# Another order of the mixer steps on three engines, with 63 filler matmuls at three steps in place of 39 at two

## The reference, cut to what matters

```python
for l in range(DEPTH):                       # DEPTH = 2
    x = x + 0.5 * swiglu(rms_norm(x, ffn1_norm[l]), ...)
    h = rms_norm(x, mix_norm[l])
    pa, pb, pc, pd = jnp.split(h @ w_in[l], IN_SPLITS, axis=-1)
    ya = neighbourhood_mixer(pa, ...)        # A: 4 heads of 64, bias table
    yb = mla_mixer(pb, ...)                  # B: low-rank q and kv, 4 heads of 96, rotary
    yc = diff_mixer(pc, ...)                 # C: 4 pairs of heads of 32, softmax1 - lambda * softmax2
    yd = gqa_mixer(pd, ...)                  # D: 4 heads of 64 over 2 kv heads, rotary
    x = x + jnp.concatenate([ya, yb, yc, yd], axis=-1) @ w_out[l]
    x = x + 0.5 * swiglu(rms_norm(x, ffn2_norm[l]), ...)
    x = rms_norm(x, final_norm[l])
```

## Time and profile before

| | |
|---|---|
| median of 3 runs | 1285.97 us (1278.35, 1285.97, 1286.76) |
| the profiled execution | 1278.74 us |
| its span in the trace | 1276.5 us |
| TensorE busy | 1242.9 us, 97% |
| VectorE busy | 847.6 us, 66% |
| ScalarE busy | 640.1 us, 50% |
| first mixer stage | 192.8 to 325.3 us |
| second mixer stage | 691.0 to 823.5 us |

### The profile page before, as it was taken

One profiled execution on the slowest core, in us unless ns is written; L12 is line 12 of the kernel. 1 busy time (PEld: TensorE's weight loads), 2 busy tenths in 40 slices (PEclk: granted clock), 3 DMA queues, 4 the chain that ended last, 5 costly groups with the idle time before them and its releaser, 6 DMA issues.

```text
span 1276.5 us, 24950 instructions
## 1 busy us (share of the span) xinstructions
PE 1242.9 (97%) x10579; PEld 1218.0 (95%) x10579; DVE 847.6 (66%) x1076; ACT 640.1 (50%) x857; POOL 79.6 (6%) x57
## 2 busy tenths in 40 slices
PE   7999999999999999999999999999999999999997
PEld 7999999889999999999999998999999999899996
DVE  6766667697766666876667678776666764446666
ACT  5343346766533334533335776643333554756543
POOL 1110011210000000000001121000000000000000
PEclk9999999999999999999999999999999999999999
DMA  8876565422466665565565532365555655324543
GB/s 286 244 227 209 197 233 155 133 100 67 136 229 197 197 197 165 179 215 189 190 219 160 167 111 68 100 220 190 188 193 197 192 180 179 119 82 155 177 150 115
DMA packets 171899, 220.34 MB, mean 173 GB/s; under 512 B 5360, under 2 KB 152560, under 8 KB 171696
## 3 DMA queue, kind: packets, MB, share of 16 engines
q1 hardware_dynamic: 168064, 213.66, 52.2%
q0 software_dynamic: 2080, 2.48, 1.1%
q10 hardware_dynamic: 1680, 3.13, 0.8%
HBM read 218.15 MB, written 3.42 MB: 174 GB/s over the span
## 4 chain that ended last, share of the span: by engine, by line
PE 86%; DVE 7%; ACT 5%; issue 2%; DMA 0%; SPq 0%; DVEq 0%; POOLq 0%; POOL 0%; ACTq 0%
PE pj L485 13%; PE pj L489 13%; PE pj L488 13%; PE acc L485 7%; PE acc L489 7%; PE acc L488 7%; PE tr L485 6%; PE tr L489 6%; PE tr L488 6%; PE acc L694 2%; ACT w_hi L974 1%; PE acc L663 1%; DVE w_lo L1291 1%; PE tr L653 1%; PE tr L686 1%
## 5 line engine op out<-in xcount | busy, mean ns | idle before, releaser
L1291 DVE TENSOR_TENSOR w_lo<-raw,w_hi 128x2048 fp32r<-128x2048 f32 (+1 forms) x205 | 457.3, 2231 | 228.2 <-ACT w_hi L974 226.6
L974 ACT ACTIVATE w_hi<-raw 128x2048 fp32r<-128x2048 f32 (+1 forms) x205 | 379.3, 1854 | 382.9 <-PE pj L485 136.4
L485 PE MATMUL pj<-hT_hi,w_hi 128*128 128x256 f32 x1056 | 294.4, 279 | 0.7 <-DVE scratch L1682 0.6
L489 PE MATMUL pj<-hT_hi,w_lo 128*128 128x256 f32 x1056 | 292.3, 277 | 0.0
L488 PE MATMUL pj<-hT_lo,w_hi 128*128 128x256 f32 x1056 | 292.2, 277 | 0.0
L485 PEld LDWEIGHTS pj<-hT_hi,w_hi 128*128 128x128 f32 x1056 | 198.5, 188 | 3.9 <-issue 2.4
L488 PEld LDWEIGHTS pj<-hT_lo,w_hi 128*128 128x128 f32 x1056 | 198.4, 188 | 0.3 <-issue 0.2
L489 PEld LDWEIGHTS pj<-hT_hi,w_lo 128*128 128x128 f32 x1056 | 198.3, 188 | 0.0
L485 PE MATMUL acc<-act_hi,w_hi 128*128 128x256 f32 x704 | 194.5, 276 | 2.9 <-issue 1.5
L488 PE MATMUL acc<-act_lo,w_hi 128*128 128x256 f32 x704 | 194.3, 276 | 0.0
L489 PE MATMUL acc<-act_hi,w_lo 128*128 128x256 f32 x704 | 194.3, 276 | 0.0
(11 more groups left out here) (223 smaller groups left out, 1872.6 us busy)
## 6 DMA issues: line engine op xcount, KB each, us to landing
raw<-in_w_in SPq DMA_DIRECT2D x47, 1024.0 KB, 5.4
raw<-in_ffn_w_down SPq DMA_DIRECT2D x44, 1024.0 KB, 5.0
raw<-in_ffn_w_gate SPq DMA_DIRECT2D x43, 1024.0 KB, 5.3
raw<-in_ffn_w_up SPq DMA_DIRECT2D x43, 1024.0 KB, 5.4
raw<-in_w_out SPq DMA_DIRECT2D x12, 1024.0 KB, 5.1
raw<-in_w_proj_a SPq DMA_DIRECT2D x4, 512.0 KB, 3.5
raw<-in_w_proj_b SPq DMA_DIRECT2D x4, 512.0 KB, 3.5
raw<-in_w_proj_c SPq DMA_DIRECT2D x4, 512.0 KB, 3.5
```

Source lines behind the costliest of these rows:

```text
L485: ins = pe.matmul(out, lhs[0], rhs[0], start=first, stop=False, **kw)
L489: return pe.matmul(out, lhs[1], rhs[0], start=False, stop=last, **kw)
L974: act.activation(w_hi[r % RING][:, 0:w], raw[r % RING][:, 0:w], ACT.Copy).then_inc(hi_set, 1)
L1291: dve.tensor_tensor(w_lo[r % RING][:, 0:w], raw[r % RING][:, 0:w], w_hi[r % RING][:, 0:w].bitcast(F32), ALU.subtract).then_inc(lo_set, 1)
```

## The change

The three tables list the same steps in another order, and `BUSY` has other entries. No step is added or dropped except fillers: 26 before `pv 4` (21 before), 10 before `probs 5` (none before), and 27 before `wout 0` (18 before), so 63 per layer in place of 39. The two layers share the tables, so 48 fillers are added in all.

```diff
-         ("latent", 0), ("proj", 6), ("proj", 2), ("probs", 0), ("latent_up", 0), ("probs", 1), ("pv", 0),
...
+         ("proj", 5), ("latent", 0), ("proj", 2), ("probs", 0), ("probs", 1), ("latent_up", 0), ("pv", 0),
...
-         ("probs", 5), ("yturn", "A"), ("pv", 5), ("score", 6), ("score", 7), ("turn", "D"), ("wout", 0),
...
+         ("probs", 5), ("yturn", "A"), ("pv", 5), ("score", 6), ("score", 7), ("wout", 0), ("turn", "D"),
...
-BUSY = {('pv', 4): 21, ('wout', 0): 18}
+BUSY = {('pv', 4): 26, ('probs', 5): 10, ('wout', 0): 27}
```

More of the change, by code:

```diff
@@ L62 @@
          ("norm", "B"), ("norm", "yA"), ("norm", "D"), ("norm", "yB"), ("norm", "yC"), ("norm", "yD")]
[L68 to L76, removed]
-             ("ahead", ("wout", 0)), ("norm", "yC"), ("score", 8), ("score", 9), ("probs", 8), ("probs", 9),
-             ("yturn", "C"), ("ahead", ("wout", 1)), ("norm", "yD"), ("yturn", "D"), ("ahead", ("wout", 2))]
@@ L79 @@
[L79 to L85, removed]
-             ("soft", 5), ("yturn", "A"), ("pv", 5), ("score", 6), ("norm", "yB"), ("score", 7), ("soft", 6),
-             ("prep", "yB"), ("soft", 7), ("pv", 6), ("pv", 7), ("yturn", "B"), ("score", 8), ("score", 9),
-             ("wadd", 0), ("norm", "yC"), ("prep", "yC"), ("ahead", ("wout", 0)), ("yturn", "C"), ("soft", 8),
-             ("soft", 9), ("ahead", ("wout", 1)), ("pv", 8), ("pv", 9), ("norm", "yD"), ("prep", "yD"), ("wadd", 1),
-             ("yturn", "D"), ("ahead", ("wout", 2))]
@@ L94 @@
-BUSY = {('pv', 4): 21, ('wout', 0): 18}
+ORDER_ACT = [("ahead", ("proj", 0)), ("proj", 0), ("ahead", ("proj", 1)), ("ahead", ("proj", 4)), ("proj", 1),
+             ("norm", "A"), ("proj", 4), ("ahead", ("proj", 3)), ("proj", 3), ("norm", "latent"),
+             ("ahead", ("proj", 6)), ("turn", "A"), ("proj", 6), ("ahead", ("proj", 5)), ("score", 0), ("score", 1),
+             ("proj", 5), ("latent", 0), ("norm", "C"), ("ahead", ("proj", 2)), ("proj", 2), ("probs", 0),
+             ("ahead", ("latent_up", 0)), ("latent_up", 0), ("probs", 1), ("turn", "C"), ("norm", "B"),
+             ("ahead", ("proj", 7)), ("score", 2), ("score", 3), ("proj", 7), ("ahead", ("proj", 8)),
+             ("ahead", ("proj", 9)), ("proj", 8), ("norm", "yA"), ("probs", 2), ("proj", 9), ("probs", 3),
+             ("turn", "B"), ("norm", "D"), ("score", 4), ("score", 5), ("probs", 4), ("probs", 5), ("yturn", "A"),
+             ("norm", "yB"), ("score", 6), ("score", 7), ("turn", "D"), ("probs", 6), ("probs", 7), ("yturn", "B"),
+             ("ahead", ("wout", 0)), ("norm", "yC"), ("score", 8), ("score", 9), ("probs", 8), ("probs", 9),
+             ("ahead", ("wout", 1)), ("yturn", "C"), ("norm", "yD"), ("ahead", ("wout", 2)), ("yturn", "D")]
@@ new lines @@
+ORDER_DVE = [("means", 0), ("ahead", ("proj", 0)), ("ahead", ("proj", 1)), ("ahead", ("proj", 4)), ("norm", "A"),
+             ("prep", "A"), ("norm", "latent"), ("ahead", ("proj", 3)), ("ahead", ("proj", 6)), ("score", 0),
+             ("score", 1), ("soft", 0), ("prep", "latent"), ("latent", 0), ("norm", "C"), ("soft", 1),
+             ("ahead", ("proj", 5)), ("prep", "C"), ("ahead", ("proj", 2)), ("ahead", ("latent_up", 0)), ("pv", 0),
+             ("pv", 1), ("score", 2), ("score", 3), ("norm", "B"), ("ahead", ("proj", 7)), ("soft", 2), ("soft", 3),
+             ("prep", "B"), ("ahead", ("proj", 8)), ("pv", 2), ("norm", "yA"), ("ahead", ("proj", 9)),
+             ("norm", "D"), ("pv", 3), ("score", 4), ("score", 5), ("prep", "D"), ("prep", "yA"), ("soft", 4),
+             ("soft", 5), ("pv", 4), ("pv", 5), ("score", 6), ("yturn", "A"), ("score", 7), ("norm", "yB"),
+             ("soft", 6), ("prep", "yB"), ("soft", 7), ("yturn", "B"), ("pv", 6), ("pv", 7), ("score", 8),
+             ("score", 9), ("norm", "yC"), ("wadd", 0), ("ahead", ("wout", 0)), ("soft", 8), ("prep", "yC"),
+             ("ahead", ("wout", 1)), ("soft", 9), ("pv", 8), ("yturn", "C"), ("pv", 9), ("norm", "yD"),
+             ("prep", "yD"), ("yturn", "D"), ("ahead", ("wout", 2)), ("wadd", 1)]
```

6 lines of the change are left out of this document (3 added, 3 removed).

## The result

The changed kernel takes 1293.37 us (median of five runs, 1292.95 to 1301.39) where the kernel before, run beside it, takes 1285.97 (1278.35 to 1286.76). The ratio is 1.0097, with a 95% interval of 1.0061 to 1.0133: slower, by about 1%. The profiled execution of the changed kernel is one of the long ones, 1300.54 us.

What follows compares the result with a forecast made beforehand. TensorE, busy 97%, was taken as the bound, with VectorE setting the pace mid-stage. Terms sum to +4.7 us per stage, +9.4 on 1278.74 (1288.1, factor 1.0074); times the median 1285.97 gives 1295 us, range 1280 to 1302.

Steps and rivals of the forecast that it cites:

- Slower by less than 1%: The forecast case for the whole kernel: 1295 us, 1291 to 1300, chance 0.50.
- Point 1: Front, up to scores 2 and 3: probs 1 waits for banks, latent_up waits less; +0.4 us, between 0 and +0.8.
- Point 2: turn B: probs 3 now stands ahead and its bank must be copied by ScalarE, +0.5; turn B starts +0.9 us late.
- Point 3: VectorE's stretch to prep yA: norm B and norm D now stand in it, so yturn A starts +2.9 us late.
- Point 4: Fillers at pv 4 and probs 5: covered by TensorE's wait for prep yA, taken as 0; uncovered 0.4 + 1.2 us.
- Points 5 and 6: yturn A to wout 0 and turn D, delay +3.5 us; then probs 6 waits for banks, +0.5, so pv 6 +4.0.
- Point 7: score 8 waits for pv 6's output behind yturn B on VectorE, +0.6 us; wout 1 waits some 0.1 for wout 0's addition.
- the signs that the prediction named: Profile signs: yturn A waits 1 us or more, starts 2 to 3.5 late; probs 1 waits; stage 137.2 us; clock 1.00.
- signs of being wrong: VectorE gaps over 2 us between first C score and prep D, no wait after the 10 fillers, or any clock fall.
- not slower: Rival: yturn A does not wait for VectorE, added VectorE work costs nothing; about -0.5 us per stage, 1285 us, chance 0.20.
- Higher runs cured by fillers: Rival: something in the mixer stages makes the slower runs and more fillers prevent it; 1288 us, chance 0.18.
- The clock falls: Rival: a longer stretch of transposes and small matmuls from turn B drops the clock; +5.4 us more per stage, 1306, chance 0.12.

Runs made afterwards that it cites:

- e1: Changed kernel with VectorE's means of slot 0 put back behind the low part of projection 0: ratio 1.0109, stage 138.07 and 137.77 us.
- e3: Changed kernel with pv 3 put back ahead of norm D and prep yA between scores 4 and 5 on VectorE: ratio 1.013, stage 139.11 and 138.77 us.
- e4: Changed kernel with the old fillers (21 at pv 4, none at probs 5, 18 at wout 0): ratio 1.0124, stage 138.71 and 142.08 us.
- e5: Changed kernel with what e1, e3 and e4 put back, all at once: ratio 1.0093, stage 135.88 and 135.73 us.
- wadd_prep: Changed kernel with VectorE's wadd 0 ahead of norm yC and prep yC directly behind that norm: ratio 1.0118, stage 138.50 and 138.19 us.
- e2: Changed kernel with the addition of wout 0 put back ahead of norm yC on VectorE: 1309.63 us, ratio 1.0212, stage 143.20 and 144.93 us.
- e7: Kernel before with no fillers at all: ratio 1.01, stage 138.65 and 136.35 us.
- before_fill_0: Kernel before with no fillers at wout 0, the 21 at pv 4 kept: ratio 1.0054, stage 136.28 and 136.45 us.
- e6: Kernel before with only the new fillers (26 at pv 4, 10 at probs 5, 27 at wout 0): ratio 1.0037, stage 133.87 and 134.07 us.
- e8: Kernel before with VectorE's means 0 moved ahead of the low part of projection 0: ratio 1.0005, stage 132.69 and 132.60 us.
- late_old: e5 with turn D also ahead of wout 0, and VectorE's yturn B and steps behind score 9 in old order: ratio 1.0064, stage 135.87 and 135.64 us.

## Why the prediction was right, and where its sum was short

Slower by less than 1% was the likeliest case of the prediction, and its 1295 stands beside a measured median of 1293.4. The sum behind it was short all the same: +4.7 per stage where 7.0 and 6.7 were measured, 9.4 in all against 13.7. Two of its terms were put at nothing or next to it, the wait for `prep A` at `turn A` and the wait for the addition at `wout 1`. That the number still came out is luck: the median of the shown runs of before, 1285.97, is of the upper level and the median of the changed kernel's is of its lower one, which took away about as much as the sum missed. By the lower levels it would have been 1278.4 + 9.5 = 1288 against 1293.

Step by step, as delay of TensorE against the kernel before. The last column is e1, where the long root of the front is taken out:

| TensorE reaches | predicted | changed kernel | e1 |
|---|---|---|---|
| turn A | 0 | +1.3 | +0.1 |
| scores 2 and 3 | +0.4 | +1.9 | +0.7 |
| turn B | +0.9 | +2.2 | +1.1 |
| yturn A | +2.9 | +4.4 | +3.2 |
| pv 6 | +4.0 | +5.4 | +4.2 |
| score 8 | +4.6 | +5.9 | +4.7 |
| wout 1 | +4.7 | +7.0 | +5.8 |
| end of the stage | +4.7 | +7.0 | +5.6 |

- **Point 1**, the front: 0.4 was predicted with a bound of 0.8. The waits of `probs 1` (0.64 for 0.8) and `latent_up` (0.53 for 0.7) are as it had them. What failed is that nothing ahead of projections 5 and 6 was priced. The prediction takes 0 for them "since their weights' low parts still end before TensorE comes to them", but what TensorE came to wait for is `prep A`: the slot put ahead of `norm A` took the slack, and `means 0`, moved one place, cost 1.2 us on top (e1). Neither move is named in the list of moves under "The change".
- **Point 2**, `turn B`: +0.9, measured +1.1 in e1. Right.
- **Point 3**, VectorE's stretch: the output of `pv 3` ends at 282.43 - 200.23 = 82.2 us, the 81 of the prediction plus the root. `yturn A` +2.9 against +3.2 in e1. Right as a sum, and the wait named `hn` L1441 is there. But as a cause it was overstated: VectorE's order is worth 1.5 of it, since the fillers and the queue of TensorE end almost together with it (e3, e4, e5).
- **Point 4**, fillers at `pv 4` and `probs 5` at nothing: right in the changed order (e4: without them `yturn A` moves by 0.02 us), and 1.2 us once the cover is gone (e5), where the prediction had 1.6. A wait of 1 us or more before `yturn A` was foretold; it is 0.67.
- **Points 5 and 6**: from `yturn A` to `pv 6` +1.1 was predicted, +1.0 measured. Right.
- **Point 7**: `score 8` +0.6, measured +0.5. The wait of `wout 1` for the addition is the second term that was mis-sized: 0.1 for 1.03. The addition now stands behind `norm yC`'s two instructions on VectorE, 0.9 us that the prediction did not put in; this move, too, is missing from the list under "The change". wadd_prep wins 1.0 us by undoing it.

With both terms the sum closes: 4.7 + 1.3 + 0.9 = 6.9 against 7.0 (6.7 in the second stage, where the wait before `wout 1` is 0.80). Both fixes together were not run; by e1 (-1.4) and wadd_prep (-1.0) alone I expect 137.1.

Of the signs that the prediction named, the wait for `hn` at `yturn A`, the wait of `probs 1`, the full clock and the unbroken work of VectorE from its first C score to `prep D` are there. Not there are the size of the first (0.67 us for 1 or more), the start of `yturn A` (4.4 us later where 2 to 3.5 were given) and the length of the stage (139.5 for 137.2). And one of its signs of being wrong came up by the letter: the ten fillers are followed by no wait. It comes one step later, behind `probs 5`, and is short, because TensorE's own queue ends almost together with VectorE.

Of the rivals, "not slower" is refuted by the ratio, and in the stage by the steps of the table. (Its -0.5 per stage needed all of the 1.13 us at `latent_up`; with the 0.43 that point 1 gives, its own terms come to +0.2.) "Higher runs cured by fillers" is refuted too: the changed kernel has the same two levels. "The clock falls" didn't happen in the changed kernel, whose slices are all full, but it is real nearby: it happened in e2, e4, e7 and before_fill_0. The added fillers are what keeps e4's wait from taking the clock; in the old order, where VectorE isn't late, the extra 24 only cost some 1.6 us (e6).

## What to carry to other kernels

In a kernel whose engines meet closely, price every moved entry by what runs beside it on the other engines, not only by its own place: here a one-place move of a 0.16 us instruction cost 1.2 us where another move had used up the slack (and 0.2 to 0.4 where it hadn't), and a repair of one wait of 1 us cost 3.7 and 5.7 in the two stages (with the clock), both through a GpSimd instruction that never was the bound. Look for the same small instruction with two durations in the trace of before; it was there, unread. And when two bounds lie side by side, undoing either alone shows next to nothing, so undo both before calling one of them innocent.

## What the runs showed of the hardware

**A GpSimd root waits out VectorE's low part.** The power instruction takes 0.72 us for two columns and 1.64 for eight. When VectorE's difference of two SBUF tensors (L1291) has started before it, it takes what is left of that instruction and then nearly its own time (0.58, 1.50 and 2.76 us in the three cases): 1.90 (e8 and the changed kernel), 3.74 (e2), and in the changed kernel this one, for norm B, with a low part from 263.48 to 265.77 beside it:

```profile
263.53 5.00 POOL L1832 TENSOR_TENSOR stat<-stat,half 128x16 f32<-128x16 f32 x1 [14.57 <-DVE stat L1282]
```

The kernel before has 2.89 us for it. Its two roots of 128x2 stood in the trace with 2.80 and 0.69 us. VectorE's instruction isn't lengthened, 2.29 us in both cases. With the root of the latent norm, 3.11 us at 226.37 in the changed kernel for 1.01 at 218.64 before, that accounts for the busier GpSimd on the page (2.1 + 2.1 + 1.2 us in each stage).

The Trainium skill (SBUF — State Buffer, SBUF: two separate sides) says that VectorE with two SBUF inputs and a GpSimd instruction that reads SBUF hold one pair of ports exclusively, and that the one that starts first keeps it for its whole length. Where VectorE starts first, this case agrees: 5.00 is 2.24 of the low part's rest and 2.76 more. Where the root starts first, it doesn't. Here the root of norm A in the kernel before starts 0.04 us ahead of a low part, and the two run side by side at about their usual lengths:

```profile
209.22 2.90 POOL L1832 TENSOR_TENSOR stat<-stat,half 128x16 f32<-128x16 f32 x1 [6.42 <-DVE stat L1282]
209.26 2.32 DVE L1291 TENSOR_TENSOR w_lo<-raw,w_hi 128x2048 fp32r<-128x2048 f32 x1
```

So only the order with VectorE first costs time here; why, the traces don't tell. By that order the root's 1.2 us in the front could have been foretold from the tables. That `turn A` would pay for them needed the slack of `prep A` as well.

**The clock.** It fell to 1.2 GHz after waits of 3.0 (e7), 2.3 (e2) and 2.5 us (e4, in one of two stages), and in before_fill_0 with none over 1.1, in a window in which TensorE was busy 4.24 of 6 us, part of it with transposes, scores and small products. With nine fillers it was busy 5.01 there and the clock stayed. The Trainium skill (TensorE: Matmul & The Clock Gate, Part 4: PE-mode transpose) says that transposes don't count as busy in the same way. A fall behind such short waits fits that, but no run here separates the transposes from the waits.

**Two paces of dense matmuls.** A feed-forward part runs at one of two paces, with a granted clock of 1.00 in both. First the changed kernel, then the kernel before, then late_old with both of its paces:

```profile
100.00:120.00 20.00, 20.00 (x172) 20.00 (x171) 12.26 (x9) 7.48 (x6) 2.48 (x3) 1.00 0.69 215
580.00:600.00 20.00, 20.00 (x179) 20.00 (x178) 12.93 (x13) 8.21 (x5) 0.00 (x0) 1.00 0.63 203
```

```profile
100.00:120.00 20.00, 20.00 (x179) 20.00 (x178) 12.95 (x13) 8.21 (x5) 2.24 (x3) 1.00 0.70 216
```

```profile
100.00:120.00 20.00, 20.00 (x172) 20.00 (x172) 11.76 (x9) 6.27 (x4) 2.49 (x3) 1.00 0.64 193
580.00:600.00 20.00, 20.00 (x172) 20.00 (x172) 11.81 (x9) 6.58 (x5) 0.00 (x0) 1.00 0.53 167
940.00:960.00 20.00, 20.00 (x179) 20.00 (x178) 12.58 (x10) 6.58 (x5) 0.00 (x0) 1.00 0.61 194
```

172 matmuls in 20 us against 179, over a part of some 160 us, is 6.5 us. The profile of late_old has it in two parts and took 1297.97 us, 12.5 more than its fastest run of 1285.46. It fits the 25 runs of the kernel before beside it, which lie at 1277.5 to 1280.3, 1284.3 to 1286.1 and 1290.5 to 1292.5: none, one or two such parts. It comes in both kernels and in code that no edit touched. In the profiles it is seen in the feed-forward part ahead of a mixer stage and holds to that part's end; shorter, it stands at the end of wadd_prep (172 matmuls from 1240 to 1260 us) and of before_fill_0. What sets it stays open.
